# Gate projection of the feed-forward layers: one 512-column matmul in place of two of 256 columns, and a sum of the halves

## What is computed

```python
def swiglu(h, w_gate, w_up, w_down):
    return (jax.nn.silu(h @ w_gate) * (h @ w_up)) @ w_down
```

## Time and profile before

| | us |
|---|---|
| median of 3 runs | 2578.29 |
| the three runs | 2573.68, 2578.29, 2581.61 |
| span of the profiled execution, first to last instruction | 2580.4 |
| its own time (which of the three runs it is, is not recorded; the nearest above its span) | 2581.61 |
| TensorE busy | 2369.4 (92% of the span) |
| VectorE busy | 1498.5 (58%) |
| ScalarE busy | 1021.1 (40%) |
| mean granted TensorE clock | 0.938 of full speed |

### The profile page before, as it was taken

One profiled execution on the slowest core, in us unless ns is written; L12 is line 12 of the kernel. 1 busy time (PEld: TensorE's weight loads), 2 busy tenths in 40 slices (PEclk: granted clock), 3 DMA queues, 4 the chain that ended last, 5 costly groups with the idle time before them and its releaser, 6 DMA issues.

```text
span 2580.4 us, 44727 instructions
## 1 busy us (share of the span) xinstructions
PE 2369.4 (92%) x17136; PEld 2203.8 (85%) x17136; DVE 1498.5 (58%) x2564; ACT 1021.1 (40%) x1670; POOL 0.2 (0%) x4
## 2 busy tenths in 40 slices
PE   5799899988798899989899999899978899998998
PEld 4687699987686799979899978799966799897998
DVE  4433177745441477836677776577766554666544
ACT  3312244414231344325544444444444544455443
POOL 0000000000000000000000000000000000000000
PEclk8898799998898899999899999899989899998999
DMA  4343179962433299844289854299842366442664
GB/s 127 91 112 102 33 251 289 290 192 83 123 83 99 77 291 292 271 127 129 85 273 291 289 165 127 86 292 286 276 114 82 115 181 185 127 132 85 194 186 131
DMA packets 553295, 436.26 MB, mean 169 GB/s; under 512 B 31824, under 2 KB 479352, under 8 KB 553080
## 3 DMA queue, kind: packets, MB, share of 16 engines
q1 hardware_dynamic: 549840, 431.35, 55.2%
q10 hardware_dynamic: 3368, 3.71, 0.5%
HBM read 433.96 MB, written 1.05 MB: 169 GB/s over the span
## 4 chain that ended last, share of the span: by engine, by line
PE 85%; DVE 7%; ACT 3%; issue 1%; DMA 1%; DVEq 1%; ACTq 1%; SPq 0%
PE bank L575 12%; PE bank L576 12%; PE bank L577 12%; PE acc L575 6%; PE acc L576 6%; PE acc L577 6%; PE bank L561 5%; PE bank L702 5%; PE acc L620 3%; PE bank L980 2%; PE bank L779 2%; PE bank L585 1%; PE bank L570 1%; PE bank L691 1%; PE bank L745 1%
## 5 line engine op out<-in xcount | busy, mean ns | idle before, releaser
L575 PE MATMUL bank<-h_hi,w_hi 128*128 128x256 f32 x2704 | 787.4, 291 | 28.1 <-DVE h_lo L1251 16.1
L576 PE MATMUL bank<-h_lo,w_hi 128*128 128x256 f32 x2704 | 774.6, 286 | 0.0
L577 PE MATMUL bank<-h_hi,w_lo 128*128 128x256 f32 x2704 | 774.1, 286 | 0.0
L1013 ACT ACTIVATE w_hi<-wslot 128x1024 fp32r<-128x1024 f32 x510 | 529.8, 1054 | 527.9 <-PE acc L577 312.6
L1429 DVE TENSOR_TENSOR w_lo<-wslot,w_hi 128x1024 fp32r<-128x1024 f32 x396 | 473.2, 1221 | 263.0 <-ACT w_hi L1013 262.8
L575 PEld LDWEIGHTS bank<-h_hi,w_hi 128*128 128x128 f32 x2704 | 527.9, 195 | 46.9 <-issue 31.9
L576 PEld LDWEIGHTS bank<-h_lo,w_hi 128*128 128x128 f32 x2704 | 529.9, 196 | 0.0
L577 PEld LDWEIGHTS bank<-h_hi,w_lo 128*128 128x128 f32 x2704 | 528.8, 196 | 0.0
L575 PE MATMUL acc<-mid_hi,w_hi 128*128 128x256 f32 x1056 | 302.2, 286 | 0.5 <-DVE mid_lo L1662 0.5
L577 PE MATMUL acc<-mid_hi,w_lo 128*128 128x256 f32 x1056 | 298.7, 283 | 0.0
L576 PE MATMUL acc<-mid_lo,w_hi 128*128 128x256 f32 x1056 | 298.7, 283 | 0.0
(11 more groups left out here) (255 smaller groups left out, 2742.9 us busy)
## 6 DMA issues: line engine op xcount, KB each, us to landing
wslot<-in_ada_w_dram SPq DMA_DIRECT2D x192, 512.0 KB, 5.8
wslot<-in_ffn_w_gate_dram SPq DMA_DIRECT2D x88, 512.0 KB, 4.7
wslot<-in_ffn_w_up_dram SPq DMA_DIRECT2D x88, 512.0 KB, 5.4
wslot<-in_ffn_w_down_dram SPq DMA_DIRECT2D x88, 512.0 KB, 3.4
wslot<-in_w_in_dram SPq DMA_DIRECT2D x72, 512.0 KB, 4.0
wslot<-in_sb_w_in_dram SPq DMA_DIRECT2D x48, 512.0 KB, 4.5
wslot<-in_w_ffn_gate_dram SPq DMA_DIRECT2D x44, 512.0 KB, 4.9
wslot<-in_w_ffn_up_dram SPq DMA_DIRECT2D x44, 512.0 KB, 5.6
```

What stands on the lines that cost most here:

```text
L575: pe.matmul(dst, w_hi[:, w, cols], hi, start=start, stop=False, skip_group_check=True)
L576: pe.matmul(dst, w_hi[:, w, cols], lo, start=False, stop=False, skip_group_check=True)
L577: return pe.matmul(dst, w_lo[:, w, cols], hi, start=False, stop=stop, skip_group_check=True)
L1013: return act.activation(dst, src, ACT.Copy)
```

## The change

The high and low parts of the activations move into one tensor, `h_parts`, in which the two parts of a tile k lie side by side, 512 columns in all. For the gate half, `two_halves` issues two matmuls for a tile in place of three: low weights times the high part (256 columns), and high weights times both parts at once (512 columns, the whole of `bank` b). Columns 256 to 511 then hold high weights times low activations and have to be added to columns 0 to 255. ScalarE copies them to `mid`, VectorE adds them to the other half from PSUM into `silu_g`, and silu now reads `silu_g`. The up half still uses `three`, but since `bank` b is full, it goes to `bank` 2, of which there is one for both values of b. So TensorE waits, before the up half of step f, for `mid` of step f-1, which was the last reader of `bank` 2. Lines below the edit move by 6 to 15: L1013 is L1024 afterwards, L1429 is L1442, L1659 is L1674.

```diff
-        h_hi = sb("h_hi", [P, KT, S], F32R)
-        h_lo = sb("h_lo", [P, KT, S], F32R)
+        h_parts = sb("h_parts", [P, KT, 2, S], F32R)
+        h_hi, h_lo = h_parts[:, :, 0, :], h_parts[:, :, 1, :]
...
+            def two_halves(n, w, cols, parts, start, stop):
+
+                pe.matmul(B(n, 0, 256), w_lo[:, w, cols], parts[:, 0, :], start=start, stop=False, skip_group_check=True)
+                return pe.matmul(B(n), w_hi[:, w, cols], parts.rearrange("p a s -> p (a s)"), start=False, stop=stop,
+                                 skip_group_check=True)
...
                             pe.wait_ge(slot_used[s], g(f"slot{s}") + f + 1)
+                            if n == 1 and not first:
+                                pe.wait_ge(sem["mid"], g("mid") + f)
                             for k in range(KT):
                                 if first and n == 0:
                                     pe.wait_ge(sem["h_parts"], g("h_parts") - KT + k + 1)
-                                mm = three(B(b, 256 * n, 256 * n + 256), 2 * b + n, slice(P * k, P * k + P),
-                                           h_hi[:, k, :], h_lo[:, k, :], k == 0, k == KT - 1)
+                                if n == 0:
+                                    mm = two_halves(b, 2 * b, k_cols(k), h_parts[:, k, :, :], k == 0, k == KT - 1)
+                                else:
+                                    mm = three(B(2, 0, 256), 2 * b + 1, k_cols(k),
+                                               h_hi[:, k, :], h_lo[:, k, :], k == 0, k == KT - 1)
...
                         act.wait_ge(sem["up_done"], g("up_done") + f + 1)
-                        act.activation(silu_g[:, b, :], B(b, 0, 256), ACT.Silu).then_inc(sem["silu_ready"], 1)
+                        copy(mid[:, b, :], B(b, 256, 512)).then_inc(sem["gate_low"], 1)
+                        act.wait_ge(sem["gate_sum"], g("gate_sum") + f + 1)
+                        act.activation(silu_g[:, b, :], silu_g[:, b, :], ACT.Silu).then_inc(sem["silu_ready"], 1)
...
+                        dve.wait_ge(sem["gate_low"], g("gate_low") + f + 1)
+                        dve.tensor_tensor(silu_g[:, b, :], mid[:, b, :], B(b, 0, 256), ALU.add).then_inc(sem["gate_sum"], 1)
                         dve.wait_ge(sem["silu_ready"], g("silu_ready") + f + 1)
-                        dve.tensor_tensor(mid[:, b, :], silu_g[:, b, :], B(b, 256, 512), ALU.mult).then_inc(sem["mid"], 1)
+                        dve.tensor_tensor(mid[:, b, :], silu_g[:, b, :], B(2, 0, 256), ALU.mult).then_inc(sem["mid"], 1)
```

More of the change, by code:

```diff
@@ L171, in ffn @@
     def ffn(ada=None, **more):
-        counts = dict(silu_ready=NF, mid=NF, mid_high=NF, mid_ready=NF, up_done=NF, down_done=NF,
+        counts = dict(gate_low=NF, gate_sum=NF, silu_ready=NF, mid=NF, mid_high=NF, mid_ready=NF, up_done=NF, down_done=NF,
                       w_high=3 * NF - 2, **slots(SLOT_FF, [NF - 1, NF - 1, NF]))
```

## The result

| | before | after |
|---|---|---|
| median, us | 2578.29 (9 runs, 2573.68 to 2584.25) | 2585.59 (9 runs, 2580.14 to 2589.47) |
| span of the profiled execution, us | 2580.4 | 2581.7 |
| its own time, us | 2581.61 | 2583.48 |
| TensorE, VectorE, ScalarE busy, us | 2369.4, 1498.5, 1021.1 | 2361.8, 1553.6, 1064.2 |
| mean granted clock | 0.938 | 0.938 |

The ratio after to before is 1.0034, with a 95% interval of 1.0021 to 1.0048. In a second comparison on another chip it was 1.0010 (1.0001 to 1.0019), 2583.05 against 2578.98 us. So the kernel became slower, by 4 to 7 us going by the medians. The forecast was 2574.0 us, 4.3 us faster. The measured time lies inside the range (2567 to 2592), on the other side of no change.

The account below looks back on a forecast made before the run. TensorE was taken to set the pace of all six layers before the change. Four ada layers at +2.0 us and two plain ones at -6.3 us summed to -4.3, from 2578.3 to 2574.0 us; range 2567 to 2592.

Parts of the forecast that it names:

- Matmuls: Gate half: a tile falls from 0.360 to 0.336 us; 168 tiles give -4.03 us per layer whose pace TensorE sets.
- rival C: Gate half: the wide matmul saves nothing, a tile stays at 0.360 us; +3.8 us, 2582.1 us; chance 0.10.
- the bounds given: Gate-half tile: 0.360 us if 512 columns cost two of 256, 0.323 if the 256-column matmul fell to its columns.
- ScalarE and VectorE: Chain in a step: from the end of the addition to `low` of the down weights 1.40 us, independent of TensorE.
- the ring: Ada layers, two steps: VectorE's work 15.21 us plus two waits of 1.40, 18.01 us against TensorE's 17.78, so VectorE sets pace.
- The last step's chain: End of plain layers: copy, addition and two steps between engines stand uncovered before `down(21)`, +0.88 us.
- The wait for `mid` at nothing: Before the up half: TensorE's wait for `mid` costs nothing, with 0.5 us spare in the ada layers.
- A: Ada layers: VectorE's loop is longer than worked, decisive from 0.15 us a step; with 0.17, +13.6 us, 2587.6; chance 0.22.
- B: Ada layers: VectorE's loop does not bind and TensorE sets the pace; -18.9 us, 2559.4 us; chance 0.10.
- The pieces without a releaser: VectorE's late starts without anyone to wait for, 0.17 us before L1412 and 0.39 before L1422, each said to count 80 times.
- D: Gate half: 512 columns cost the 0.120 us of 256, a tile 0.240 us; 2541.8 us; chance 0.02.

Follow-up runs that it names:

- the kernel without sum: Changed kernel with silu reading columns 0 to 255 from PSUM, copy and addition removed, so high weights times low activations is left out; 2576.34 us, ratio 0.9986 to before.
- the kernel with the chain alone: Changed kernel with the 512-column matmul split into two of 256, weights loaded for each; copy, addition and banks stay; 2588.43 us, ratio 1.0033 to before.
- the doubled addition: VectorE's addition done twice, the extra result unused: in the changed kernel 2616.49 us, in the one with unwidened steps 0 and 21 and early addition 2578.42 us.
- the reordered kernels: Changed kernel with copy and addition moved earlier: in every step 2602.58 us, not in step 0 2576.33, also with steps 0 and 21 as before the change 2577.94.
- the mixed one: Changed kernel with early copy and addition, but steps 0 and 21 use three matmuls and silu from PSUM, no sum; 2577.94 us, ratio 0.9991 to before.
- the four reorderings: Changed kernel with addition early: with copy 2602.58 us; same except step 0 2576.33; also steps 0 and 21 as before the change 2577.94; VectorE's addition only 2667.84.
- the kernel with both halves early: Changed kernel with VectorE's addition ahead of its two `low` and ScalarE's copy between the gate and up roundings, in every step; 2602.58 us, ratio 1.0081 to before.

## Why the prediction was wrong

Against the +4.7 us of the trace (4.4 in the second one) the forecast had -4.3. Two terms failed.

**"Matmuls": the tile at 0.336 us.** The step that failed is "I read 0.120 as a floor per load and matmul that the columns do not fill". It rested on a true row, that at half clock 256 columns cost 0.213 us and nothing besides. The conclusion that a cost at full clock must then be a floor was not the only one, and its premise ("if a fixed cost were added to the columns, half clock would show it too") is false here. At full clock the columns of this format cost 0.443 ns and a matmul 0.007 us more. At half clock 256 and 512 columns take 0.213 and 0.427 us, 1/1.2 ns a column and nothing besides. What full clock costs beyond 1/2.4 ns a column does not show there. The 0.216 us for 512 columns came from other formats, and this one takes 0.233 to 0.235. Tile 0.353, between forecast and rival C's 0.360 and within the bounds given. Over 168 tiles, 0.017 us each, and two plain layers this is +5.8 us. A plain layer measures -0.15 us, and by its parts -1.07 (the kernel without sum) and +0.90 (the kernel with the chain alone). The Trainium skill (TensorE: Matmul & The Clock Gate, section Back-to-back issue gap) gives N/2.4 + 2.5 ns as the gap of an isolated matmul, which is an estimate of 0.109 and 0.216 us for 256 and 512 columns. The rows here have 0.120 and 0.235: the rule does not hold for this format at either width.

**"ScalarE and VectorE": 1.40 us where 1.44 stands.** Silu was priced by its row from PSUM, and after the change it reads SBUF. Its 0.04 us in each of 20 steps is +0.8 us for a layer whose pace the ring sets, 3.2 us for four. The first ada layer gives 0.9 us back: VectorE's steps take 18.00 us, since its idle time before the store into `mod` is 0.30 us there and 0.39 in the others. TensorE's 18.05 is the longer pace there, but VectorE runs behind and ends the layer, so its path counts.

Together: -4.3 + 5.8 + 3.2 - 0.9 = +3.8 us; the traces have +4.7 and +4.4. The remaining 0.6 to 0.9 us, half of it in the fourth layer (+1.71, where the corrected terms give +1.3), is unexplained. In that layer it stands behind `down(21)`, where 0.9 us are added and 0.5 in the others.

**What was right.** VectorE's path sets the ada layers and TensorE's gain is lost there: the wide matmul alone brings -1.07 us an ada layer, copy and addition on top of it cost 2.31 in the mean, and the doubled addition costs 0.33 us a step in the one order and nothing in the other. Where it is lost was not as told: the prediction has TensorE idle "about 0.1 us a step" before the gate half, and the steps show 0.02, while most of the loss stands at `down(21)` and behind it. The last step's chain: +0.88 forecast, +0.90 measured. The wait for `mid` at nothing: shown in the plain layers, not tried in the ada layers.

**The rivals.** A said that the ring is longer than worked and named pieces of 0.17 to 0.39 us a step. The direction was right, the size 0.04 us a step, far below the 0.15 from which it was to decide. The pieces without a releaser that it named are in the ring, but had already been counted in the 15.21 us; and each of them stands once in two steps (9 times in 905 to 1070 us), so 40 times and not 80. B (TensorE's pace in ada layers) is what the reordered kernels show, not this one. C (the wide matmul saves nothing, +3.8 us) comes closest in its number, and was nearly true: 0.007 of the hoped 0.024 us a tile. D is out. The chances had the time within 0.3% at 0.58; by the trace the change is 0.17 to 0.18%, by the first comparison 0.34%, by the second 0.10%. That the time lies in the range is luck: A set its slow end, with pieces that are not the cause.

**What stays open.** The traces' 4.4 and 4.7 us lie between the two measured ratios (7.3 and 4.1 us by medians). Outside the feed-forward layers the traces scatter by several us (1375.7 us before, 1372.2 and 1374.0 after, 1379.5 without sum), partly with how long the half clock lasts at the start of a stage. Whether the first comparison's surplus is of that kind was not settled. No kernel that computes the whole came out measurably faster than before. Of these the mixed one is the best by the stretches of its trace, 5.7 us or 0.2%, which would need more runs.

## What to carry to other kernels

Price a matmul in its own number format and at the clock at which it will run: half clock does not show the per-column cost at full clock, and 512 columns of one format say little of another. Before a step is put into a chain between two in-order engines, add up the ring that it closes, and compare it with the busiest engine's pace: at 18.05 against 18.09 us every hundredth counts. Then ask which engine ends the loop: most of the loss here stood in the last step and not in the pace. The busiest engine's busy share of 100% does not show that it waits. When a step is moved forward in a queue, look at what it waits for in the first pass of the loop and at what then stands behind it; of the four reorderings here two ran 24 and some 90 us longer than before, most of it by that.

## What the runs showed of the hardware

- A matmul in fp32r with a load of its own: at full clock 0.120, 0.175 and 0.233 to 0.235 us from start to start for 256, 384 and 512 columns, hence 0.443 ns a column and 0.007 us each. At half clock the columns cost 1/1.2 ns and nothing besides. TensorE, first step of a plain layer, after:

```profile
2029.17 0.63 PE L582 MATMUL bank<-h_parts,w_hi 128*128 128x512 f32 x1
2029.60 0.57 PE L581 MATMUL bank<-h_parts,w_lo 128*128 128x256 f32 x1
```

  0.43 us for 512 columns, which is 512/1.2 = 0.427. So full clock gives a factor of 1.82 for 512 columns, not 2.
- ScalarE's silu of 128x256 took 0.42 us from SBUF and 0.38 from PSUM, and the instruction behind it started 0.32 and 0.28 us after it.
- At the start of a feed-forward layer the half clock lasted 3.2 to 3.4 us in some executions and 6.0 to 6.5 in others of the same kernel. The third start of the changed kernel took 14.77 us with 6.5 us of half clock and 13.70 with 3.4. It is not the only cause of scatter: others took 14.4 us with 3.4 of half clock.
- A wait of TensorE of 2.1 us (2.34 us between two starts) was followed by 3.4 us of half clock in three of the six starts of the kernel with both halves early.
